# Forget-gate bias of an attention stage: carried to every partition by DMA and a DRAM scratch instead of by matrix products

## What is computed

```python
def fox_attention(q, k, v, log_f):
    ...
    c = jnp.cumsum(log_f.astype(jnp.float32), axis=1).transpose(0, 2, 1)
    ...
    def block(args):
        i, q_i, c_i = args
        scores = jnp.einsum('bqhd,bkhd->bhqk', q_i, k).astype(jnp.float32) * scale
        bias = c_i[..., :, None] - c[..., None, :]
        q_pos = i * Q_BLOCK + jnp.arange(Q_BLOCK)
        causal = key_pos[None, :] <= q_pos[:, None]
        logits = jnp.where(causal, scores + bias, -jnp.inf)
        p = jax.nn.softmax(logits, axis=-1)
        return jnp.einsum('bhqk,bkhd->bqhd', p.astype(v.dtype), v)
```

## Time and profile before

| | us |
|---|---|
| median of 3 runs | 1263.84 (1263.52 to 1264.38) |
| profiled execution, its own time | 1263.06 |
| its span | 1261.3 |
| TensorE matmul busy | 1225.0 (97%) |
| TensorE weight load busy | 1085.6 (86%) |
| VectorE busy | 769.4 (61%) |
| ScalarE busy | 608.1 (48%) |
| GpSimd busy | 0.2 |
| mean DMA rate | 172 GB/s |

### The profile page before, as it was taken

How to read it: one execution, slowest core, us unless ns; L and a number is a source line. 1 busy time by engine, 2 the same in 40 slices (tenths; PEclk the granted TensorE clock), 3 DMA queues, 4 the chain that set the end, 5 groups by cost and what they waited for, 6 DMA issues and landing times.

```text
span 1261.3 us, 18443 instructions
## 1 busy us (share of the span) xinstructions
PE 1225.0 (97%) x7568; PEld 1085.6 (86%) x7568; DVE 769.4 (61%) x851; ACT 608.1 (48%) x677; POOL 0.2 (0%) x4
## 2 busy tenths in 40 slices
PE   5999999999999999999999999999999999999997
PEld 4979998888888789999899778999989977899895
DVE  5566875674465665555456787555575578755555
ACT  4555555555454454444365445444436544545441
POOL 0000000000000000000000000000000000000000
PEclk9999999999999999999999999999999999999999
DMA  5644344444565446554353453655535345465550
GB/s 205 229 179 141 127 167 152 170 147 150 206 214 184 164 167 215 186 196 170 134 201 134 142 202 142 232 193 187 179 134 201 135 142 200 144 225 187 186 191 33
DMA packets 32957, 217.31 MB, mean 172 GB/s; under 512 B 3840, under 2 KB 5888, under 8 KB 7168
## 3 DMA queue, kind: packets, MB, share of 16 engines
q1 hardware_dynamic: 32896, 216.44, 48.2%
HBM read 215.37 MB, written 1.05 MB: 172 GB/s over the span
## 4 chain that ended last, share of the span: by engine, by line
PE 82%; DVE 9%; DMA 4%; ACT 3%; issue 2%; SPq 0%; ACTq 0%; DVEq 0%
PE gps L1293 32%; PE gps L1332 7%; PE aps L1332 7%; PE aps L1333 7%; PE aps L1338 7%; PE gps L1333 7%; PE gps L1338 7%; DMA raw<-w 4%; DVE w_lo L727 3%; ACT w_hi L329 2%; PE aps L1451 1%; DVE B L881 1%; DVE rs L871 1%; DVE B L875 1%; DVE B L825 1%
## 5 line engine op out<-in xcount | busy, mean ns | idle before, releaser
L727 DVE TENSOR_TENSOR w_lo<-raw,w_hi 128x2048 fp32r<-128x2048 f32 x196 | 448.3, 2291 | 281.9 <-ACT w_hi L329 281.2
L329 ACT ACTIVATE w_hi<-raw 128x2048 fp32r<-128x2048 f32 x196 | 373.9, 1911 | 222.2 <-DMA raw<-w 110.2
L1293 PE MATMUL gps<-R_hi,w_hi 128*128 128x256 f32 x736 | 192.5, 283 | 0.0
L1293 PE MATMUL gps<-R_hi,w_lo 128*128 128x256 f32 x736 | 192.3, 283 | 0.0
L1293 PE MATMUL gps<-H_hi,w_hi 128*128 128x256 f32 x640 | 171.1, 289 | 5.9 <-ACT H_hi L364 5.7
L1293 PE MATMUL gps<-H_hi,w_lo 128*128 128x256 f32 x640 | 167.9, 284 | 0.0
L1332 PE MATMUL aps<-w_hi,Q_hi 128*128 128x512 f32 x416 | 162.6, 391 | 1.6 <-DVE Q_lo L931 1.0
L1333 PE MATMUL aps<-w_lo,Q_hi 128*128 128x512 f32 x416 | 162.2, 390 | 0.0
L1293 PE MATMUL gps<-R_lo,w_hi 128*128 128x256 f32 x736 | 147.6, 283 | 0.0
L1293 PEld LDWEIGHTS gps<-R_hi,w_lo 128*128 128x128 f32 x736 | 141.2, 192 | 0.8
L1293 PEld LDWEIGHTS gps<-R_hi,w_hi 128*128 128x128 f32 x736 | 141.1, 192 | 0.8
(11 more groups left out here) (214 smaller groups left out, 1431.8 us busy)
## 6 DMA issues: line engine op xcount, KB each, us to landing
raw<-w SPq DMA_DIRECT2D x196, 1024.0 KB, 4.8
B<-rows SPq DMA_DIRECT2D x4, 1024.0 KB, 5.0
B<-x_t SPq DMA_DIRECT2D x2, 512.0 KB, 4.7
B<-mem_t SPq DMA_DIRECT2D x1, 1024.0 KB, 8.6
B<-x SPq DMA_DIRECT2D x1, 1024.0 KB, 7.0
B<-con SPq DMA_DIRECT2D x1, 1024.0 KB, 8.8
out<-B SPq DMA_DIRECT2D x4, 256.0 KB, 2.0
B<-rows SPq DMA_DIRECT2D x1, 512.0 KB, 6.7
```

The source lines that it names most:

```text
L329: act.activation(w_hi[:, ring(l), :], raw[:, raw_slot(l), :], ACT.Copy)\
L727: dve.tensor_tensor(w_lo[:, ring(l), :], raw[:, raw_slot(l), :], w_hi[:, ring(l), :].bitcast(F32), ALU.subtract)\
L1293: return pe.matmul(gps[:, bank_, nt * T:(nt + 1) * T], w[:, r, c:c + P], op[:, k, :], start=start, stop=stop, skip_group_check=True)
```

## The change

- `decays` is now 8 x 256 and is neither copied, rounded nor split: the copy, `decays_hi`, `decays_lo`, `picks` and the four products per head pair are gone.
- SyncE, between the loads of halves 5 and 6 of each layer, waits for the running sum, stores it (8 KB) in a DRAM scratch `turns`, waits for that, and loads it back spread over all 128 partitions twice: all 256 keys of 8 heads into `B6` (1 MB), and the first 128 keys into `past_bias` in `sqh` (0.5 MB).
- GpSimd adds the causal block to `B6` in place, in two instructions of four heads each (`f_bias`).
- VectorE's one addition per pair becomes two: the two diagonal blocks with `bias`, the block of past keys with `past_bias`. For c = 0 and c = 2 it waits for GpSimd.

```diff
--- before.py
+++ after.py
@@ -72,7 +72,7 @@
         self.eng.wait_ge(self.sem, self.base + self.n)
 
 
-def build(nc, mem_t, x_t, x, w1, w2, rows1, rows2, rows3, par1, par2, con1, con2, out):
+def build(nc, mem_t, x_t, x, w1, w2, rows1, rows2, rows3, par1, par2, con1, con2, turns, out):
     with ExitStack() as ctx:
         def sb(name, shape, dt=F32):
             return ctx.enter_context(nc.sbuf_tensor(name, shape, dt))
@@ -149,10 +149,9 @@
         causal = con[:, C_CAUSAL:C_CAUSAL + 384]
         gate_rows = soft[0:FOX_HEADS, 0, 0:T]
         gate_tmp = soft[0:FOX_HEADS, 1, 0:T]
-        decays = rs[:, :, :].rearrange("p a t -> p (a t)")[0:FOX_HEADS, 256:640]
-        picks = R_lo[0:FOX_HEADS, 0:4, :].rearrange("p a t -> p (a t)").rearrange("p (h q) -> p h q", h=FOX_HEADS)
-        decays_hi = R_hi[0:FOX_HEADS, 0:2, :].rearrange("p a t -> p (a t)")[:, 0:384]
-        decays_lo = R_hi[0:FOX_HEADS, 2:4, :].rearrange("p a t -> p (a t)")[:, 0:384]
+        decays = rs[:, :, :].rearrange("p a t -> p (a t)")[0:FOX_HEADS, 256:512]
+        bias = B6[:, :, :].rearrange("p h (t k) -> p h t k", t=2)
+        past_bias = sqh[:, :, :].rearrange("p a (h k) -> p (a h) k", h=4)
         fl = spb[:, 0, :, :]
         fpt = spb[:, 1, :, :]
 
@@ -171,7 +170,7 @@
             cx_s cx_max cx_exp cx_p cx_t cx_pt cx_o cx_oe ox_hi ox_lo
             mg mg_tr mg_hi mg_lo ffn_relu ffn_sq ffn_hi hidden
             wf_hi_ready wf_lo_ready f_mm f_gate
-            f_pick f_sp f_decay f_dhi f_dlo fx_s fx_l fx_max fx_e fx_p fx_t fx_pt fx_o fx_ohi fx_oe
+            f_sp f_decay f_out f_in f_bias fx_s fx_l fx_max fx_e fx_p fx_t fx_pt fx_o fx_ohi fx_oe
             rt_mm rt_x rg_sig rg_t rn_s rn_m rn_o gn_v gn_log gn_r gn_n gn_y gn_tr gn_hi gn_lo""".split()
         s = {n: sem(n) for n in names}
         block = ctx.enter_context(nc.Block())
@@ -286,7 +285,14 @@
                                  rows2[2 * ly + i:2 * ly + i + 1, :].to_broadcast([P, 2 * D]))\
                       .then_inc(s["rows_loaded"], 16)
 
-                for i in range(1, 8):
+                for i in range(1, 3):
+                    load_pair(i)
+                sp.wait_ge(s["f_decay"], ly + 1)
+                sp.dma_start(turns[ly], decays).then_inc(s["f_out"], 16)
+                sp.wait_ge(s["f_out"], 16 * (ly + 1))
+                sp.dma_start(B6[:, :, :], turns[ly:ly + 1].to_broadcast([P, FOX_HEADS, T])).then_inc(s["f_in"], 16)
+                sp.dma_start(past_bias, turns[ly:ly + 1, :, 0:P].to_broadcast([P, FOX_HEADS, P])).then_inc(s["f_in"], 16)
+                for i in range(3, 8):
                     load_pair(i)
                 sp.wait_ge(s["fx_l"], 4 * ly + 4)
                 sp.dma_start(gn_row, rows3[ly:ly + 1, :].to_broadcast([P, 4 * P])).then_inc(s["gn_row_loaded"], 16)
@@ -450,9 +456,6 @@
 
                 if n < LAYERS:
                     split(h0, l0 + 32)
-                    act.wait_ge(s["gemm_done"], h0 + (l0 + 28))
-                    act.activation(picks, ident[0:FOX_HEADS, 0:FOX_HEADS].unsqueeze(2)
-                                   .to_broadcast([FOX_HEADS, FOX_HEADS, P]), ACT.Copy).then_inc(s["f_pick"], 1)
                     split(h0, l0 + 33)
                     split_gates(n)
 
@@ -672,9 +675,6 @@
                     elif l == LRV + 1:
                         for m in range(2):
                             evac(rv[:, m, :], bank(LRV + 2 + m), done)
-                    if l == LFQ:
-                        act.wait_ge(s["f_decay"], ly + 1)
-                        act.activation(decays_hi, decays, ACT.Copy).then_inc(s["f_dhi"], 1)
                     if 6 <= l <= 12 and l % 2 == 0:
                         fox_out((l - 6) // 2)
                     if 5 <= l <= 11 and l % 2 == 1:
@@ -1146,22 +1146,20 @@
                     dve.wait_ge(s["f_sp"], ly + 1)
                     st.mark(dve.scalar_tensor_tensor(gate_tmp, gate_rows, 0.0, gate_tmp, ALU.min, ALU.subtract))
                     st.settle()
-                    st.mark(dve.tensor_tensor_scan(decays[:, 128:384], one_col[0:FOX_HEADS, :].to_broadcast([FOX_HEADS, T]),
-                                                   gate_tmp, 0.0, ALU.mult, ALU.subtract))
-                    st.settle()
-                    dve.tensor_copy(decays[:, 0:128], decays[:, 128:256]).then_inc(s["f_decay"], 1)
-
-                def fox_decays_lo():
-                    dve.wait_ge(s["f_dhi"], ly + 1)
-                    dve.wait_ge(s["f_decay"], ly + 1)
-                    dve.tensor_tensor(decays_lo, decays, decays_hi.bitcast(F32), ALU.subtract)\
-                       .then_inc(s["f_dlo"], 1)
+                    dve.tensor_tensor_scan(decays, one_col[0:FOX_HEADS, :].to_broadcast([FOX_HEADS, T]),
+                                           gate_tmp, 0.0, ALU.mult, ALU.subtract).then_inc(s["f_decay"], 1)
 
                 def fox_max(c):
                     dve.wait_ge(s["fx_s"], ly * 4 + c + 1)
                     if c >= 1:
                         dve.wait_ge(s["fx_t"], ly * 4 + c)
-                    dve.tensor_tensor(fl, aps[:, 0:2, 0:384], causal.unsqueeze(1).to_broadcast([P, 2, 384]), ALU.add)\
+                    if c % 2 == 0:
+                        dve.wait_ge(s["f_bias"], ly * 2 + c // 2 + 1)
+                    heads = slice(2 * c, 2 * c + 2)
+                    scores = aps[:, 0:2, 0:384].rearrange("p h (t k) -> p h t k", t=3)
+                    masked = fl.rearrange("p h (t k) -> p h t k", t=3)
+                    dve.tensor_tensor(masked[:, :, 0:3:2, :], scores[:, :, 0:3:2, :], bias[:, heads, :, :], ALU.add)
+                    dve.tensor_tensor(masked[:, :, 1, :], scores[:, :, 1, :], past_bias[:, heads, :], ALU.add)\
                        .then_inc(s["fx_l"], 1)
                     dve.wait_ge(s["fx_l"], ly * 4 + c + 1)
                     top = small[:, 3, 4 * c:4 * c + 4]
@@ -1207,8 +1205,6 @@
 
                     if l == LFV + 1:
                         fox_decays()
-                    if l == LFQ:
-                        fox_decays_lo()
                     if 4 <= l <= 10 and l % 2 == 0:
                         fox_max((l - 4) // 2)
                     if 6 <= l <= 12 and l % 2 == 0:
@@ -1280,6 +1276,19 @@
                 if more:
                     for a in range(2):
                         split(g0, p + HALVES2 + LFQ + a)
+
+
+        @block.gpsimd
+        def _(pool):
+
+            block_mask = causal[:, 0:P].unsqueeze(1).unsqueeze(1)
+            pool.wait_ge(s["con_loaded"], 16)
+            for ly in range(LAYERS):
+                pool.wait_ge(s["f_in"], 32 * (ly + 1))
+                for i in range(2):
+                    heads = slice(4 * i, 4 * i + 4)
+                    pool.tensor_tensor(bias[:, heads, :, :], bias[:, heads, :, :],
+                                       block_mask.to_broadcast([P, 4, 2, P]), ALU.add).then_inc(s["f_bias"], 1)
 
 
         @block.tensor
@@ -1612,16 +1621,7 @@
                         q, k = (b[64 * hh:64 * hh + 64, c, :] for b in (fq, fk))
                         pe.matmul(aps[:, hh, 0:128], q[:, 0:128], k[:, 0:128], start=True, stop=False,
                                   skip_group_check=True)
-                        pe.matmul(aps[:, hh, 128:384], q[:, 128:256], k, start=False, stop=False,
-                                  skip_group_check=True)
-                    if c == 0:
-                        pe.wait_ge(s["f_pick"], ly + 1)
-                        pe.wait_ge(s["f_dlo"], ly + 1)
-                    for hh in range(2):
-                        pick = picks[:, 2 * c + hh, :]
-                        pe.matmul(aps[:, hh, 0:384], pick, decays_hi, start=False, stop=False,
-                                  skip_group_check=True)
-                        ins = pe.matmul(aps[:, hh, 0:384], pick, decays_lo, start=False, stop=True,
+                        ins = pe.matmul(aps[:, hh, 128:384], q[:, 128:256], k, start=False, stop=True,
                                         skip_group_check=True)
                     ins.then_inc(s["fx_s"], 1)
 
@@ -1876,6 +1876,7 @@
     args = [nc.dram_tensor(k, v.shape, mybir.dt.from_np(v.dtype), kind="ExternalInput").ap()
             for k, v in arrays.items()]
     out = nc.dram_tensor("out", (T, D), F32, kind="ExternalOutput").ap()
-    build(nc, *args, out)
+    turns = nc.dram_tensor("turns", (LAYERS, FOX_HEADS, T), F32, kind="Internal").ap()
+    build(nc, *args, turns, out)
     r = run(nc, [arrays], core_ids=[0])
     return np.ascontiguousarray(r.results[0]["out"]).reshape(1, T, D)
```

## The result

| | before | changed |
|---|---|---|
| median over all runs, us | 1263.5 (1260.42 to 1266.0) | 1268.59 (1264.64 to 1270.48) |
| ratio, 95% interval | | 1.0040 (1.0033 to 1.0047) |
| profiled execution / its span, us | 1263.06 / 1261.3 | 1264.64 / 1262.9 |

The change costs 5.1 us (4.2 to 5.9). The profiled execution of the changed kernel is the lowest of its 17. One reason can be seen: the drop of TensorE's clock at 82 to 86 us that the earlier trace rows show is missing in it, so its first running sum ends at 641.34 and not at 643.29. Times are therefore compared from the running sum on. From the first running sum to the second it takes 318.3 us where before took 316.4, and from there to the end 303.9 for 302.3.

A forecast was written before the change was run, and what follows sets the result against it. TensorE was taken to bound the kernel (82% of the chain). First layer +2.6, second +3.0, clock +1.0 make +6.6 us on 1263.06, so 1269.7, or 1270.5 from the median; range 1265.2 to 1276.

The forecast's parts named there:

- the prediction's slack of 0.5 us: First pair on VectorE: its scaling ended 0.5 us before TensorE came to the transposes, so its addition could start that late.
- Store: SyncE's 8 KB store of the running sum: 2.0 us, kept from the nearest row, a 256 KB store.
- Half 6 and half 7: Weight loads behind the spreading loads, first layer: landing at 655.1 and 657.6; bounds for half 7 1.4 us earlier, 1.6 later.
- First pair: VectorE's addition behind half 7's split, first layer: 5.7 us late, TensorE resuming 5.3 us late; second layer 6.1 us late.
- Copy-out wait: TensorE at the first scores, waiting for ScalarE's copy-out of half 3 from 654.33 to 657.5: 3.2 us.
- Transposes' wait: TensorE, after scores and half 5's products, waits again for the first pair's scaling before the transposes: about 3 us.
- the clock term: TensorE's clock drop after new waits: nothing behind the first, 1.7 us behind the second; bounds 0 and 3.4, taken 1.0.
- Gain, 3 x 0.89 per layer: TensorE's four forget products per pair removed: 0.89 us each at pairs 2 to 4, 2.7 us; the first pair's vanishes.
- GpSimd, nothing on the chain: GpSimd's two additions, 1.15 us each to 9 us as bounds, fit the window before VectorE asks: nothing on the chain.
- Cheap spreading loads: Rival: spreading loads cost next to nothing, SyncE is late only by the store; -2.7 us, about 1261.1; chance 0.14.
- The whole gain: Rival: half 7 still lands by 651.9, nothing is late, 8 x 0.89 less 0.2 is won: 1257 us; chance 0.04.
- GpSimd as the brake: Rival: GpSimd's two additions take over 4.5 us, holding VectorE's splits; at 4 us each +6.6 more, 1277; chance 0.08.

The follow-up runs named there:

- 1 no transfers: Changed kernel without the store of the running sum and both spreading loads, GpSimd starting at the running sum: 1259.83 us for 1263.43 before, ratio 0.9975.
- 2 store only: Changed kernel with the store and SyncE's wait for it, but without the two spreading loads: 1260.24 us for 1263.43 before, ratio 0.9976.
- 3 no GpSimd: Changed kernel without GpSimd's two additions per layer, VectorE waiting for the transfers alone: 1268.63 us for 1263.43 before, ratio 1.0039.
- 6 store, no GpSimd: Changed kernel with the store and its wait, but without spreading loads and GpSimd's additions: 1260.26 us for 1262.89 before, ratio 0.9980.
- 7 half 6 first: Changed kernel with half 6 loaded before SyncE waits for the running sum, half 7 still behind the spreading loads: 1271.82 us for 1262.89 before.
- 8 placed: Changed kernel with half 6 loaded first, one 1 MB spreading load, GpSimd adding by pairs in VectorE's idle time: 1267.64 us for 1262.89 before.
- 9 store first: As 8 placed, but the store is issued ahead of half 6's load and waited for behind it: 1265.53 us for 1263.07 before, ratio 1.0025.
- 11 change, store first: Changed kernel with only half 6's load moved between the store and the wait for it, both spreading loads kept: 1271.32 us for 1263.07 before.
- experiment 4: Kernel before, products kept, with the three transfers added and their data used by nothing: 1273.15 us for 1263.43 before, ratio 1.0077.
- experiment 5: Changed kernel with neither the three transfers nor GpSimd's additions: 1256.74 us for 1262.89 before, ratio 0.9949.
- the tenth: As 9 store first, but VectorE splits half 7 after the first pair's scaling, not ahead of its additions: 1263.33 us for 1263.07 before, ratio 1.0001.

## Why the prediction was right, point by point

**The sum.** Forecast +6.6 us, slower; measured +5.1. The sum of one layer can be set up anew for each kernel. *Late* is by how much the first pair's additions start later after the running sum's start than before's 13.52 us; *slow* is the time of the six transposes and half 6's 48 products over before's 0.66 + 5.74; 0.4 is the prediction's slack of 0.5 us less 0.1 for the second addition; the gain is 3 x 0.89 = 2.67. The sum should be by how much TensorE comes later, from the running sum's end, to the last pair's transposes. The chains have them, before and changed:

```profile
708.78 0.68 PE aps L1634 x6
...
708.23 0.77 PE aps L1634 x6
```

These are 65.49 and 66.89 us behind 643.29 and 641.34, so 1.40 late. The first layer of each kernel in which TensorE waits for the first pair and no later one; the last column goes on to the second running sum (before: 316.35):

| kernel | late | slow | late + slow - 0.4 - gain | TensorE late at last pair | late at second running sum |
|---|---|---|---|---|---|
| changed | 4.26 | 0.21 | +1.40 | +1.40 | +2.0 |
| 1 no transfers | 0.84 | 0.21 | -2.02 | -2.03 | -1.5 |
| 2 store only | 0.93 | 0.21 | -1.93 | -1.94 | -1.4 |
| 3 no GpSimd | 4.23 | 0.22 | +1.38 | +1.38 | +1.8 |
| 6 store, no GpSimd | 0.93 | 0.23 | -1.91 | -1.94 | -0.9 |
| 7 half 6 first | 4.83 | 2.21 | +3.97 | +3.97 | +4.5 |
| 8 placed | 2.76 | 1.67 | +1.36 | +1.37 | +1.9 |
| 9 store first | 1.76 | 1.77 | +0.46 | +0.45 | +0.9 |
| 11 change, store first | 3.70 | 2.57 | +3.20 | +3.19 | +3.9 |

Nothing above 0.03 us is left at the last pair, so the form of the sum holds. For the second layer of the changed kernel it gives 4.67 late (17.78 against 13.11) + 0.23 - 0.4 - 2.67 = +1.83 (measured: +1.82). The two layers make 3.2 us, where the forecast had 2.6 + 3.0, and 1.0 for the clock. Behind the last pair every traced run with an edit, experiment 4 too, loses another 0.4 to 1.0 us against the traced run of before; that is no term of the sum, and its cause was not traced. The sizes of the terms were off as follows.

- **Store, forecast 2.0 us:** 1.32. The row of 256 KB was too long for 8 KB, as feared. The Trainium skill (DMA: Bandwidth & Descriptors, section Anatomy of one DMA — SWDGE (gpsimd) path) puts the fixed part of a DMA at about 2.0 us for another path; this store stayed under it.
- **Half 6 and half 7, forecast to land 11.8 and, of the running sum's end, 14.3 us behind:** half 6 came 10.5 us behind it (651.81 - 641.34) and half 7 12.9, as in the prediction's lower bound. Of the 1.4 us, 0.7 are the store. The four queued transfers of the earlier trace rows were not too dear: there the fourth was issued 2.2 us after the first and landed 10.0 us later; here the fourth was issued 1.6 us after the first and landed 9.9 later.
- **First pair, forecast 5.7 us late, TensorE back 5.3 late:** 4.26 and 3.9 (transposes at 663.94 against 662.03, each from the end of its own running sum). In the second layer 4.67, forecast 6.1, and TensorE 4.3.
- **Copy-out wait, forecast 3.2 us:** 1.9 and 2.5. **Transposes' wait, forecast about 3 us:** 1.3 in each layer. It is shorter because the slow stretch of the clock fell in front of it; with those 1.5 us it would have been as forecast. The prediction had this case right ("nothing behind the first"), and that decided much: the clock term, taken at 1.0, came to nothing that shows. The 0.2 us per layer in the column *slow* stand also in experiments 1 and 6, where the clock did not fall.
- **Gain, 3 x 0.89 per layer:** borne out by experiment 5 and the table, roughly by experiment 4.
- **GpSimd, nothing on the chain:** right; 2.36 us for each addition, where the estimate from the Trainium skill's GPSIMD Engine Reference was 2.25. The rule on the shared port held too: the split that began at 653.76, before GpSimd was done at 654.12, took 2.51 us by the chain, and experiment 1 shows the rule in full.

**Rivals.** *Cheap spreading loads* fell with experiments 2 and 3: with the store alone the kernel gains 3.2 us, the loads take 8 back. *The whole gain* is experiment 5, the kernel that the transfers' delay excludes. *GpSimd as the brake* fell with experiment 3. Its own condition was met (4.72 us for the pair, over 4.5; 2.36 us each, over 2.2), but GpSimd began 8.1 us behind the sum's end and not 9.3, and half 6's split was held up for 0.22 us only. It would need VectorE to have work when GpSimd starts.

Of the measured +5.1 the two layers explain 3.2, half of the forecast 6.6. That the total came out nearer is in part luck, for the other 1.9 us are no term of the sum. The changed kernel's trace, of its fastest execution, has only some of them: +2.0 between the running sums and +1.6 from the second one to the end. The trace of experiment 3, whose stages are the same, shows +4.4 from there to the end. The 2.8 us between these two arise from 1094 to 1127 us, in the feed-forward part behind the layers, which no edit touches. In experiment 3's trace a weight load landed there some 1.2 us later against the running sum, TensorE had a wait that the changed kernel's does not have, and its clock fell behind it (columns as in the earlier trace rows):

```profile
PE aps L1328 <- DVE Q_lo L931: 1.9, 1, 1.9
```

```profile
1097.90:1101.90 4.00, 2.12 (x8) 1.55 (x8) 3.97 (x6) 3.23 (x4) 0.00 (x0) 0.89 0.63 207
1101.90:1105.90 4.00, 4.00 (x14) 3.17 (x13) 3.08 (x4) 2.34 (x2) 0.00 (x0) 0.68 0.55 174
```

Whether the untraced executions of the changed kernel lose time in the same way, and whether the change makes that likelier, stays open. In the other experiments the two layers of the trace and the difference of the medians also lie up to 1.9 us apart, either way (experiment 4: 11.6 and 9.7).

Of the kernels that leave nothing out, none beats the one before by a measurable amount; the tenth equals it. Issuing the store or the spreading loads from ScalarE's queue, and a third buffer for the weights, were not tried.

## What to carry to other kernels

Before small data is carried by DMA in a kernel whose weights stream on the same queue, name the loads that it pushes back and follow each through the in-order engines to the first deadline: here 3.6 us of products per layer, 2.7 of which could still count, was worth less than 4.3 us of lateness in a supply with 0.5 us of slack. When one wait is removed from a pair of waits, ask what the wait that remains was hiding; and when an in-order engine's list is reordered to meet one deadline, look for the buffer that the postponed instruction frees.

## What the runs showed that was not expected

- **A small DMA takes the time of what stands ahead of it on its queue.** The 8 KB store took 1.32 us on an empty queue, 1.34 with a 1 MB load issued behind it, and 4.05 and 3.95 with that load issued 1 us ahead (first layers; the second ones agree). The Trainium skill (DMA: Bandwidth & Descriptors, section Queues, rings and completion order) says that each DMA engine consumes descriptors in ring order, and these four agree with it.
- **Where the clock falls matters as much as whether.** Where it fell between two waits it cost nothing that shows (changed kernel, experiment 3: *slow* is 0.2 us, as in experiments 1 and 6 without a fall). Where no wait followed, the column *slow* has 1.7 to 2.6 us per layer (experiments 7 to 9 and 11 and the second layer of 2; so has the first layer of experiment 4, where the clock fell behind the second of two waits). Two experiments (7 and 11) that removed the first wait cost 8.9 and 8.3 us where the changed kernel cost 5.1. A single wait was not dear by itself: behind waits of 1.2 to 1.9 us in experiments 1 and 6 and the first layer of 2 the clock stayed at 1.00. It stayed behind 1.75 and 1.87 us, and fell behind 1.74, 1.88 and 1.92, so these runs do not say what wait it takes.
- **GpSimd beside VectorE:** two splits lengthened by 1.73 and 1.16 us, GpSimd's own pair by 2.09.
